# One projection tile for the attention keys instead of two, and the RWKV bonus sums issued earlier

## The chip, the cores and the metric

The kernel runs on one core of one Trainium2 chip. The time is the device time of one execution in microseconds (us); what is compared is the median over several executions. Engines are named as in the profile: PE is TensorE's matmul stream and PEld its weight loads, DVE is VectorE, ACT is ScalarE, POOL is GpSimd, and SP is the engine that here only issues DMAs.

## What is computed

The reference is one layer of a hybrid decoder on 512 tokens of width 1024. Cut to what matters here:

```
mod  = silu(c) @ ada_w + ada_b            # shift, scale and gate of both sub-layers
h    = x * (1 + scale1) + shift1
proj = h @ w_in                           # q 512 | k 128 | v 128 | rwkv r, k, v 3*512 | three loras 256
y_attn = sliding_window_attention(q, k, v)      # 8 heads of 64, grouped on 2 key/value heads
y_rwkv = rwkv7(...)                       # 8 heads of 64, ends in:
    bonus = sum(r * k * r_k, over the 64 of a head) * v
    y     = (group_norm(state output) + bonus) * g
x = LayerNorm(alpha * x + gate1 * (concat(y_attn, y_rwkv) @ w_out))
...                                       # then a PEER layer: top-16 of 128*128 experts, 8 heads
```

The keys have 128 columns, 64 for each of the two key/value heads. Heads of attention come in pairs on the two halves of the 128 partitions, so the score matmuls need each key head on both halves.

## The kernel before, in words

The program has three stages, each begun by an all-engine barrier: `emit_projections` (barrier L270, from 3 us), `emit_mixing` (barrier L881, from 192 us: attention and the RWKV recurrence) and `emit_experts` (barrier L1716, the rest). The change touches the first alone.

**Projection tiles.** `w_in` is worked off in TILES = 21 tiles of 128 columns, in this order: 14 RWKV tiles (j = 0 to 13), the values (j = 14, V_TILE), four query tiles (15 to 18, Q_TILE) and two key tiles (19 and 20, K_TILE). A key tile holds the 64 columns of one key head twice, loaded by two DMAs, so that its product has this head on both halves of the partitions. A tile is computed in split precision: SP loads `wt` (L294, or L290 for keys), ACT rounds it to `wth` (L429), DVE forms the remainder `wtl` (L721), and PE adds three times eight matmuls of 128x128x512: `wth` with `hi` (L563), `wth` with `lo` (L573), `wtl` with `hi` (L568). ACT copies the result out of its PSUM bank (L443 RWKV, L446 values, L448 queries, L450 keys); for RWKV tiles DVE then mixes it with the token before (L727). The three result banks are 0, 1 and 7.

**What is woven in.** The order on each engine is written out by hand, as `if j == ...` branches in the loop over tiles. An engine goes through its instructions in order, and semaphores tie the engines together. Near the change stand:

- *Key norms.* POOL squares `KN` (L385), PE sums the squares per head into bank 4 (`squares`, L595, at j = 13 and 14), DVE puts a floor under them (L761), ACT takes the root (L494, at j = 15), DVE the reciprocal (L818, at j = 16), and PE spreads the result to the rows of two pairs at j = 16 and of two at j = 17 (`norm_rows`, L606, banks 3 and 5). DVE's `normalised(p)` has three operations per pair of heads (L774, L777, L781).
- *Bonus.* POOL multiplies r and k (L391) into `tmp[2 + p % 2]`, two buffers for four pairs of heads p; DVE scales by `r_k` (`bonus_in`, L765); PE sums over each head (`bonus`, L615, banks 4 and 5), which are two matmul records per pair of heads; DVE multiplies by v (`bonus_out`, L770). PE issues `bonus` 0 and 1 at j = 18 and 2 and 3 behind the last tile.
- *Products with the decays.* Behind L391 POOL has four products for k (L396) and four for `AI` (L399), and DVE has four for r at j = 20 (L833).
- *Modulation of the second sub-layer.* DVE adds `ada_b` to 16 columns of bank 6 (L838, L839) behind its loop.

The two waits of POOL and PE around the bonus:

```
pool.wait_ge(bsum_up, START + p - 1)              # POOL, before the product of p = 2, 3 (L390)
pe.wait_ge(nk_up, START + 2 * (PAIRS - 1) + 1)    # PE, before bonus: banks 3 and 5 read (L612)
```

Of the kernel before, what the change touches and what calls it, by code (L numbers as in the profile page):

```python
# [8 lines left out]
P = 128  # L9
# [4 lines left out]
PAIRS = HEADS // 2  # L14
ATTN_COLS = 768
# [4 lines left out]
START = 8  # L20
# [172 lines left out]
def emit_projections(nc, banks, sem, v):  # L193
# [10 lines left out]
    with ctx:  # L204
# [23 lines left out]
        vT = asum[0]  # L228
        xin = [[qT[:, 2 * t + h, :] for h in range(2)] for t in range(2)] + [tmp[0:2], tmp[2:4]]
# [10 lines left out]
        gb_in, sink_in = sem("gb_in"), sem("sink_in")  # L240
# [25 lines left out]
        Q_TILE = V_TILE + 1  # L266
        K_TILE = Q_TILE + 4
        TILES = K_TILE + 2

# [4 lines left out]
        def _(sp):  # L274
# [9 lines left out]
            def weights(j):  # L284
                if j >= 2:
                    sp.wait_ge(wtl_up, START + j - 1)
                if j >= K_TILE:
                    n = j - K_TILE
                    for d in range(2):
                        sp.dma_start(wt[j % 2][:, :, 64 * d:64 * d + 64], wv[:, :, 512 + 64 * n:576 + 64 * n])\  # L290
                            .then_inc(wt_in[j % 2], 16)
                    return
                at = (ATTN_COLS + RWKV[j] * P if j < V_TILE else 640 if j == V_TILE else (j - Q_TILE) * P)
                sp.dma_start(wt[j % 2][:, :, :], wv[:, :, at:at + P]).then_inc(wt_in[j % 2], 16)  # L294
# [20 lines left out]
            for j in range(3, TILES):  # L315
                weights(j)
                if j in (5, 7, 9, 11):
                    ada_load((j + 7) // 2)
            sp.wait_ge(gb_in, START + 32)
# [3 lines left out]
        def _(pool):  # L323
# [63 lines left out]
            for p in range(PAIRS):  # L387
                pool.wait_ge(kp_up, START + PAIRS + p + 1)
                if p >= 2:
                    pool.wait_ge(bsum_up, START + p - 1)  # L390
                pool.tensor_tensor(tmp[2 + p % 2][:, :], PM[:, p, :], PM[:, 4 + p, :], ALU.mult).then_inc(rk_up, 1)  # L391
# [10 lines left out]
        def _(act):  # L402
# [22 lines left out]
            def rounded(j):  # L425
                act.wait_ge(wt_in[j % 2], START + 16 * (j // 2 + 1) + (16 if j >= K_TILE else 0))
# [11 lines left out]
            def evacuated(j):  # L438
                act.wait_ge(proj_up, START + j + 1)
                src = slots[j % 3][:, :]  # L440
                if j < V_TILE:
                    n = RWKV[j]
                    act.activation(PM[:, n, :], src, ACT.Copy, scale=omu[:, n:n + 1]).then_inc(proj_scaled, 1)  # L443
                elif j == V_TILE:
                    act.wait_ge(ada_used, START + len(pieces))
                    act.activation(vT[:, :], src, ACT.Copy).then_inc(proj_scaled, 1)  # L446
                elif j < K_TILE:
                    act.activation(qT[:, j - Q_TILE, :], src, ACT.Copy, scale=HD ** -0.5).then_inc(proj_scaled, 1)  # L448
                else:
                    act.activation(kT[:, j - K_TILE, P:], src, ACT.Copy).then_inc(proj_scaled, 1)  # L450

# [48 lines left out]
        def _(pe):  # L500
# [108 lines left out]
            def bonus(p):  # L609
                pe.wait_ge(rks_up, START + p + 1)  # L610
                pe.wait_ge(ss_max, START + 1)
                pe.wait_ge(nk_up, START + 2 * (PAIRS - 1) + 1)  # L612
                if p >= 2:
                    pe.wait_ge(bo_up, START + p - 1)
                pe.matmul(banks[4 + p % 2][:, :], diag2[:, :], tmp[2 + p % 2][:, :], start=True, stop=True)\  # L615
                    .then_inc(bsum_up, 1)
# [18 lines left out]
            for j in range(TILES):  # L635
# [10 lines left out]
                elif j == 16:  # L646
# [6 lines left out]
                    norm_rows(1)  # L653
                elif j == 17:
                    norm_rows(2)
                    norm_rows(3)
                elif j == 18:
                    bonus(0)
                    bonus(1)
            bonus(2)  # L660
            bonus(3)

        @block.vector
        def _(dve):
# [98 lines left out]
            def bonus_in(p):  # L763
                dve.wait_ge(rk_up, START + p + 1)
                dve.tensor_scalar(tmp[2 + p % 2][:, :], tmp[2 + p % 2][:, :], par[:, R_RK + p:R_RK + p + 1], None,  # L765
                                  ALU.mult).then_inc(rks_up, 1)

            def bonus_out(p):
                dve.wait_ge(bsum_up, START + p + 1)
                dve.tensor_tensor(BO[:, p, :], banks[4 + p % 2][:, :], PM[:, 8 + p, :], ALU.mult).then_inc(bo_up, 1)  # L770
# [22 lines left out]
            for j in range(TILES):  # L793
# [16 lines left out]
                elif j == 15:  # L810
                    floored()
                    bonus_in(0)
                    bonus_in(1)
                elif j == 16:
# [3 lines left out]
                    dve.reciprocal(norms, norms).then_inc(norms_up, 1)  # L818
                elif j == 17:
                    normalised(0)  # L820
                    normalised(1)
                elif j == 18:
                    normalised(2)
                    normalised(3)
                elif j == 19:
                    bonus_out(0)
                    bonus_in(2)
                    bonus_out(1)
                    bonus_in(3)
                elif j == 20:  # L830
# [1688 lines left out]
```

## Time and profile before

| | us |
|---|---|
| median of 3 runs (lowest, highest) | 1800.62 (1797.14, 1803.17) |
| the profiled execution | 1799.91 |
| its span, first to last instruction | 1798.2 |
| first projection tile starts on PE | 43.5 |
| barrier between projections and mixing is released | 192.1 |
| mean granted TensorE clock of the core | 0.987 |

The profiled execution's time is 1.7 us above its span, and 0.7 us below the median. A timeline row gives the start in us, the time until the end of the merged instructions, the engine, the line, the operation, the tiles it writes and reads, their count, and in brackets how long the engine sat idle before it and what ended that. PE's matmuls are pipelined, so that a row's time reaches a little into the next one's: starts are the surer measure.

### The profile page before, as it was taken

Reading aid. Unit: us, or ns where it says so; the run is one execution under the profiler, and the core shown is the slowest. Engines: PE = TensorE matmul, PEld = TensorE weight load, DVE = VectorE, ACT = ScalarE, POOL = GpSimd, SP = SyncE. Lnnn points to the kernel's source line nnn. Section 1 sums busy time; section 2 is a strip of 40 time slices with the busy share of each in tenths; the row PEclk is TensorE's granted clock in tenths of the full one; section 3 lists DMA queues with packets and bytes.
Section 4 is the critical chain, followed back from the end, with each engine's and each line's share of the span. In section 5 each row is a group of like instructions: output and inputs, shape, how many; then the busy total and the mean of one; then the engine's idle time right before and its main releaser. Section 6 shows DMA issues by size and latency. Waiting matters only on the chain.

```text
span 1798.2 us, 36538 instructions
## 1 busy us (share of the span) xinstructions
PE 1731.4 (96%) x12400; PEld 1515.6 (84%) x12400; DVE 1412.4 (79%) x2928; ACT 695.4 (39%) x1304; POOL 603.5 (34%) x481
## 2 busy tenths in 40 slices
PE   5999899889999999899999999999999999999996
PEld 3776788747999999899999999999888888888885
DVE  1885666646878888899999999687698888888877
ACT  3433455514444454433333333334343333333331
POOL 5012633303344353444333343353243332233200
PEclk8999999999999999999999999999999999999998
DMA  9841000254443434699999998999999999999981
GB/s 318 278 155 48 2 3 3 79 202 163 129 135 122 129 123 127 238 321 322 322 327 348 321 317 307 326 411 368 367 412 349 358 351 350 357 357 349 349 281 63
DMA packets 247871, 444.37 MB, mean 247 GB/s; under 512 B 85522, under 2 KB 158580, under 8 KB 247780
## 3 DMA queue, kind: packets, MB, share of 16 engines
q1 hardware_dynamic: 207968, 300.07, 48.0%
q0 software_dynamic: 39168, 142.62, 21.2%
q8 instruction: 50, 0.82, 0.2%
q10 hardware_dynamic: 644, 0.52, 0.2%
q14 instruction: 41, 0.34, 0.1%
HBM read 388.16 MB, written 54.53 MB: 246 GB/s over the span
## 4 chain that ended last, share of the span: by engine, by line
PE 73%; DMA 2%; DVE 1%; SPq 1%; ACT 1%; issue 0%; ACTq 0%; POOL 0%; DVEq 0%
PE bank L1489 26%; PE bank L2030 10%; PE bank L2031 10%; PE bank L2032 10%; PE bank L1469 6%; PE bank L1952 5%; PE bank L2009 4%; PE bank L1427 2%; DMA vsel<-in_peer_v,picks 1%; PE bank L1964 1%; SPq L1460 1%; DMA xrows<-xpicks 0%; DMA uraw<-in_peer_u,xrows 0%; DMA urows<-in_peer_u 0%; DVE n_stats L1393 0%
## 5 line engine op out<-in xcount | busy, mean ns | idle before, releaser
L1489 PE MATMUL bank<-hh,uh 128*128 128x368 f32 x1024 | 350.4, 342 | 0.0
L1489 PE MATMUL bank<-hl,uh 128*128 128x368 f32 x1024 | 337.4, 329 | 0.0
L2030 PE MATMUL bank<-vh,wh 128*128 128x512 f32 x768 | 299.8, 390 | 3.1 <-DVE wl L2443 3.1
L2031 PE MATMUL bank<-vl,wh 128*128 128x512 f32 x768 | 299.6, 390 | 0.0
L2032 PE MATMUL bank<-vh,wl 128*128 128x512 f32 x768 | 299.6, 390 | 0.0
L1547 POOL DMA_INDIRECT vsel<-in_peer_v,picks x128 | 154.2, 1204 | 406.8 <-DVE gt L1573 392.5
L2183 ACT ACTIVATE vh<-vraw 128x1024 fp32r<-128x1024 f32 x128 | 135.9, 1062 | 285.7 <-PE bank L2032 269.6
L1547 POOL DMA_INDIRECT wide<-in_peer_u,picks x108 | 152.6, 1413 | 202.3 <-DVE wide L1554 188.1
L2440 DVE TENSOR_TENSOR vl<-vraw,vh 128x1024 fp32r<-128x1024 f32 x128 | 156.5, 1223 | 80.2 <-ACT vh L2183 80.2
L1489 PEld LDWEIGHTS bank<-hl,uh 128*128 128x128 f32 x1024 | 193.1, 189 | 0.0
L1489 PEld LDWEIGHTS bank<-hh,uh 128*128 128x128 f32 x1024 | 192.8, 188 | 0.0
L1489 PE MATMUL bank<-hh,ul 128*128 128x368 f32 x1024 | 192.5, 330 | 0.0
L1489 PEld LDWEIGHTS bank<-hh,ul 128*128 128x128 f32 x1024 | 174.6, 189 | 0.0
L1573 DVE SCALAR_TENSOR_TENSOR gt<-vsel,wsel,gt 128x1024 f32<-128x1024 f32 x128 | 164.1, 1282 | 13.0 <-DMA vsel<-in_peer_v,picks 5.5
L2030 PEld LDWEIGHTS bank<-vh,wh 128*128 128x128 f32 x768 | 144.5, 188 | 33.5 <-DVE vl L2440 3.5
L2032 PEld LDWEIGHTS bank<-vh,wl 128*128 128x128 f32 x768 | 144.6, 188 | 30.0
L2031 PEld LDWEIGHTS bank<-vl,wh 128*128 128x128 f32 x768 | 144.7, 188 | 29.9
L1512 POOL TENSOR_TENSOR ul<-uraw,uh 128x1024 fp32r<-128x1024 f32 x41 | 99.1, 2416 | 189.6 <-ACT uraw L1504 189.6
L2162 ACT ACTIVATE SS<-bank 128x512 f32<-128x512 f32 x96 | 57.5, 599 | 254.8 <-PE bank L2009 254.8
L1497 ACT ACTIVATE uh<-bank 128x512 fp32r<-128x512 f32 x256 | 144.9, 607 | 25.3 <-PE bank L1469 14.2
L1520 DVE TENSOR_TENSOR ul<-bank,uh 128x512 fp32r<-128x512 f32 x174 | 111.7, 683 | 45.4 <-ACT uh L1497 45.0
L1469 PE MATMUL bank<-ident,urows 128*128 128x128 f32 x1024 | 133.2, 273 | 3.8 <-DVE ul L1520 1.6
(379 smaller groups left out, 2989.1 us busy)
## 6 DMA issues: line engine op xcount, KB each, us to landing
urows<-in_peer_u SPq DMA_DIRECT2D x128, 512.0 KB, 8.2
vraw<-in_peer_v SPq DMA_DIRECT2D x128, 512.0 KB, 6.3
scored<-act_out SPq DMA_DIRECT2D x128, 192.0 KB, 5.2
gates<-SS SPq DMA_DIRECT2D x16, 1536.0 KB, 14.7
gtile<-gates SPq DMA_DIRECT2D x32, 768.0 KB, 7.5
act_in<-scored SPq DMA_DIRECT2D x128, 192.0 KB, 6.3
wt<-in_w_in SPq DMA_DIRECT2D x19, 512.0 KB, 4.4
wq<-in_peer_wq SPq DMA_DIRECT2D x18, 512.0 KB, 3.9
```

Source lines behind the costliest of these rows:

```text
L1469: last = pe.transpose(self.banks[2 + h][:, k * P:(k + 1) * P], self.u[s][:, (4 * h + k) * P:(4 * h + k + 1) * P], self.ident[:, :])
L1489: last = pe.matmul(bank, u[:, k, :], h[:, k, 0:TU], start=(n == 0), stop=(n == 3 * KD - 1))
L1497: act.activation(self.uh[s % 2][:, 4 * h:4 * h + 4, :], self.banks[2 + h][:, :].rearrange("p (k e) -> p k e", k=4), ACT.Copy)\
L1512: pool.tensor_tensor(self.ul[s % 2][:, :, :], self.uraw[:, :, :], self.uh[s % 2][:, :, :].bitcast(F32), ALU.subtract).then_inc(self.ul_up, 1)
L1520: dve.tensor_tensor(self.ul[s % 2][:, 4 * h:4 * h + 4, :], self.banks[2 + h][:, :].rearrange("p (k e) -> p k e", k=4), self.uh[s % 2][:, 4 ...
L1547: pool.indirect_dma_start(out=into[:, :], out_offset=None, in_=row, in_offset=bass.IndirectOffsetOnAxis(ap=self.picks[:, at:at + 1], axis=0))\
L1573: dve.scalar_tensor_tensor(out=self.y[:, :], in0=self.vsel[k][:, :], scalar=self.wsel[:, k:k + 1], in1=self.y[:, :], op0=ALU.mult, op1=ALU ...
L2030: pe.matmul(b, wh[s][:, cols], vh[s][:, half], start=first, stop=False)
L2031: pe.matmul(b, wh[s][:, cols], vl[s][:, half], start=False, stop=False)
L2032: last = pe.matmul(b, wl[s][:, cols], vh[s][:, half], start=False, stop=stop)
L2183: act.activation(vh[s][:, :], vraw[s][:, :], ACT.Copy).then_inc(vh_up, 1)
L2440: dve.tensor_tensor(vl[s][:, :], vraw[s][:, :], vh[s][:, :].bitcast(F32), ALU.subtract)\
```

## The change

- The keys become one tile of 128 columns, at j = 15, ahead of the four query tiles; there are 20 tiles. ACT writes the product's lower half to head 0's place and its upper half to head 1's place in `kT`, in two instructions of 64 partitions. When both are written, SP copies each to the other half of the partitions by a DMA of 64 partitions x 512 values, and waits for both DMAs before the barrier.
- The products of r and k go to four buffers `rk` (tmp 2, 3, 0, 1). POOL's product for p = 2 and 3 no longer waits for a bonus sum, but for the sums of squares that read tmp 0 and 1.
- The bonus sums go to banks 4 and 6. PE issues 0 and 1 at j = 16, behind `norm_rows` 0 and 1, and 2 and 3 at j = 18. DVE's parts move along: the modulation of bank 6 to j = 15, `bonus_in` 2 and 3 to j = 16, `bonus_out` to j = 17 and 18, and the products of r with the decays from j = 20 to j = 19.

```diff
+        rk = tmp[2:4] + tmp[0:2]
-        Q_TILE = V_TILE + 1
-        K_TILE = Q_TILE + 4
-        TILES = K_TILE + 2
+        K_TILE = V_TILE + 1
+        Q_TILE = K_TILE + 1
+        TILES = Q_TILE + 4
...
 SP: weights(j)
-                if j >= K_TILE:
-                    n = j - K_TILE
-                    for d in range(2):
-                        sp.dma_start(wt[j % 2][:, :, 64 * d:64 * d + 64], wv[:, :, 512 + 64 * n:576 + 64 * n])\
-                            .then_inc(wt_in[j % 2], 16)
-                    return
...
+            sp.wait_ge(proj_scaled, START + K_TILE + 1)
+            for n in range(2):
+                here, other = (slice(64 * d, 64 * d + 64) for d in (n, 1 - n))
+                sp.dma_start(kT[other, n, P:], kT[here, n, P:]).then_inc(k_in, 16)
+            sp.wait_ge(k_in, START + 32)
             sp.wait_ge(gb_in, START + 32)
...
 POOL
                 if p >= 2:
-                    pool.wait_ge(bsum_up, START + p - 1)
-                pool.tensor_tensor(tmp[2 + p % 2][:, :], PM[:, p, :], PM[:, 4 + p, :], ALU.mult).then_inc(rk_up, 1)
+                    pool.wait_ge(ss_up, START + p + 1)
+                pool.tensor_tensor(rk[p][:, :], PM[:, p, :], PM[:, 4 + p, :], ALU.mult).then_inc(rk_up, 1)
...
 ACT: evacuated(j)
+                elif j == K_TILE:
+                    act.activation(kT[0:64, 0, P:], slots[j % 3][0:64, :], ACT.Copy)
+                    act.activation(kT[64:P, 1, P:], slots[j % 3][64:P, :], ACT.Copy).then_inc(proj_scaled, 1)
...
 PE: bonus(p), and the loop
-                pe.wait_ge(nk_up, START + 2 * (PAIRS - 1) + 1)
+                pe.wait_ge(cols_used, START + 3)
-                pe.matmul(banks[4 + p % 2][:, :], diag2[:, :], tmp[2 + p % 2][:, :], start=True, stop=True)\
+                pe.matmul(banks[4 + 2 * (p % 2)][:, :], diag2[:, :], rk[p][:, :], start=True, stop=True)\
...
                     norm_rows(1)
+                    bonus(0)
+                    bonus(1)
                 elif j == 17:
                     norm_rows(2)
                     norm_rows(3)
                 elif j == 18:
-                    bonus(0)
-                    bonus(1)
-            bonus(2)
-            bonus(3)
+                    bonus(2)
+                    bonus(3)
...
 DVE: the loop
                     bonus_in(1)
+                    dve.wait_ge(ada_used, START + 8)
+                    dve.tensor_tensor(mod[:, 16:32], banks[6][:, 16:32], par[:, R_ADAB + 24:R_ADAB + 40], ALU.add)\
+                        .then_inc(cols_used, 1)
+                    dve.wait_ge(cols_used, START + 3)
+                    dve.tensor_scalar(mod[:, 24:32], mod[:, 24:32], 1.0, None, ALU.add)
                 elif j == 16:
...
+                    bonus_in(2)
+                    bonus_in(3)
                 elif j == 17:
                     normalised(0)
                     normalised(1)
+                    bonus_out(0)
+                    bonus_out(1)
                 elif j == 18:
                     normalised(2)
                     normalised(3)
+                    bonus_out(2)
+                    bonus_out(3)
                 elif j == 19:
-                    bonus_out(0)
-                    bonus_in(2)
-                    bonus_out(1)
-                    bonus_in(3)
-                elif j == 20:
                     dve.wait_ge(rk_up, START + PAIRS)
                     for p in range(PAIRS):
                         dve.tensor_tensor(PM[:, p, :], PM[:, p, :], PD[:, p, :], ALU.mult)
...
-            step(dve.tensor_tensor(mod[:, 16:32], banks[6][:, 16:32], par[:, R_ADAB + 24:R_ADAB + 40], ALU.add))
-            dve.tensor_scalar(mod[:, 24:32], mod[:, 24:32], 1.0, None, ALU.add)
-            bonus_out(2)
-            bonus_out(3)
```

## Rows read from the trace of the kernel before

**Rows 1.** Busy time by stretch: us, engines busy (x instructions), PEclk, DMA, GB/s
```profile
45.00:188.00 143.00, 141.84 (x587) 105.72 (x586) 111.41 (x138) 51.00 (x66) 26.17 (x20) 0.98 0.48 151
188.00:192.00 4.00, 1.68 (x4) 0.38 (x2) 1.94 (x3) 0.59 (x1) 2.98 (x3) 1.00 0.00 0
192.00:340.00 148.00, 138.55 (x3455) 120.44 (x3456) 93.23 (x177) 82.96 (x213) 60.36 (x73) 1.00 0.01 3
```

**Rows 2.** Timeline, PE in the last two tiles
```profile
178.72 1.98 PE L573 MATMUL bank<-lo,wth 128*128 128x512 f32 x8
...
184.16 1.98 PE L573 MATMUL bank<-lo,wth 128*128 128x512 f32 x8
...
185.97 1.98 PE L568 MATMUL bank<-hi,wtl 128*128 128x512 f32 x8
```

**Rows 3.** Timeline, end of the stage, all engines
```profile
185.11 5.87 POOL L399 TENSOR_TENSOR AI<-AI,wide 128x512 f32<-128x512 f32 x4
...
187.79 1.88 PE L615 MATMUL bank<-tmp,diag 128*128 128x512 f32 x4
187.99 0.60 ACT L450 ACTIVATE kT<-bank 128x512 f32<-128x512 f32 x1 [4.85 <-PE bank L568]
...
189.71 0.69 DVE L770 TENSOR_TENSOR BO<-bank,PK 128x512 f32<-128x512 f32 x1 [0.17 <-PE bank L615]
...
192.16 1.05 POOL L932 TENSOR_TENSOR BHs<-AI,PL 128x512 f32<-128x512 f32 x1 [1.17 <-POOLq L881]
```

**Rows 4.** Waits of POOL, 28 to 197 us: in total, times, longest
```profile
POOL tmp L391 <- PE bank L615: 33.3, 1, 33.3
```

**Rows 5.** Timeline around tile 16, ACT, DVE and PE
```profile
151.51 0.60 ACT L448 ACTIVATE qT<-bank 128x512 f32<-128x512 f32 x1 [5.96 <-PE bank L568]
152.00 1.05 ACT L429 ACTIVATE wth<-wt 128x1024 fp32r<-128x1024 f32 x1
...
154.37 0.63 ACT L494 ACTIVATE rn<-rn 8x512 f32<-8x512 f32 x1
...
155.03 3.34 DVE L818 RECIPROCAL rn<-rn 8x512 f32<-8x512 f32 x1 [0.61 <-ACT rn L494]
...
156.76 0.60 PE L650 MATMUL bank<-ident,asum 128*128 128x128 f32 x4
...
158.51 1.95 PE L606 MATMUL bank<-rn,g 8*128 8x512 f32 x4 [1.16 <-DVE rn L818]
...
160.40 3.47 PE L563 MATMUL bank<-hi,wth 128*128 128x512 f32 x8
...
165.77 1.99 PE L568 MATMUL bank<-hi,wtl 128*128 128x512 f32 x8
```

**Rows 6.** Busy time by stretch, columns as in rows 1
```profile
162.00:164.00 2.00, 2.00 (x6) 1.62 (x5) 1.78 (x3) 0.00 (x0) 0.00 (x0) 0.50 0.00 0
```

**Rows 7.** Timeline, the first pair of bonus sums
```profile
171.55 1.98 PE L573 MATMUL bank<-lo,wth 128*128 128x512 f32 x8
...
175.18 1.88 PE L615 MATMUL bank<-tmp,diag 128*128 128x512 f32 x4
...
176.24 0.69 DVE L770 TENSOR_TENSOR BO<-bank,PK 128x512 f32<-128x512 f32 x1 [1.55 <-PE bank L615]
```

**Rows 8.** Timeline, second pair of sums of squares on PE
```profile
143.90 1.88 PE L595 MATMUL bank<-tmp,head_of 128*8 128x512 f32 x4
```

**Rows 9.** Products on DVE and POOL by line: ns min/median/max, first to last start
```profile
L833 DVE TENSOR_TENSOR PK<-PK,PD x4: 1770/1776/1778, 180.5 to 185.6; 128x512 f32<-128x512 f32 x4
...
L781 DVE TENSOR_TENSOR PK<-PK,wide x4: 691/691/695, 161.1 to 174.0; 128x512 f32<-128x512 f32 x4
...
L396 POOL TENSOR_TENSOR PK<-PK,wide x4: 1480/1610/1750, 178.8 to 183.4; 128x512 f32<-128x512 f32 x4
```

**Rows 10.** SP's last weight issues, and the landing of all 23 loads of `wt`
```profile
146.83 8.50 SPq L290 DMA_DIRECT2D wt<-in_w_in  x4
...
DMA to landing us min/median/max: 3.1/4.4/15.9
```

More of the change, by code:

```diff
@@ L239, in emit_projections @@
         wt_in = [sem(f"wt_in{i}") for i in range(2)]
-        gb_in, sink_in = sem("gb_in"), sem("sink_in")
+        gb_in, sink_in, k_in = sem("gb_in"), sem("sink_in"), sem("k_in")
         consts, rows_up, par_up, silu_up = sem("consts"), sem("rows_up"), sem("par_up"), sem("silu_up")
@@ L286, in weights @@
                     sp.wait_ge(wtl_up, START + j - 1)
-                if j >= K_TILE:
-                    n = j - K_TILE
-                    for d in range(2):
-                        sp.dma_start(wt[j % 2][:, :, 64 * d:64 * d + 64], wv[:, :, 512 + 64 * n:576 + 64 * n])\
-                            .then_inc(wt_in[j % 2], 16)
-                    return
-                at = (ATTN_COLS + RWKV[j] * P if j < V_TILE else 640 if j == V_TILE else (j - Q_TILE) * P)
+                at = (ATTN_COLS + RWKV[j] * P if j < V_TILE else {V_TILE: 640, K_TILE: 512}.get(j, (j - Q_TILE) * P))
                 sp.dma_start(wt[j % 2][:, :, :], wv[:, :, at:at + P]).then_inc(wt_in[j % 2], 16)
@@ L425, in rounded @@
             def rounded(j):
-                act.wait_ge(wt_in[j % 2], START + 16 * (j // 2 + 1) + (16 if j >= K_TILE else 0))
+                act.wait_ge(wt_in[j % 2], START + 16 * (j // 2 + 1))
                 if j >= 3:
@@ L446, in evacuated @@
                     act.activation(vT[:, :], src, ACT.Copy).then_inc(proj_scaled, 1)
-                elif j < K_TILE:
+                elif j == K_TILE:
+                    act.activation(kT[0:64, 0, P:], slots[j % 3][0:64, :], ACT.Copy)
+                    act.activation(kT[64:P, 1, P:], slots[j % 3][64:P, :], ACT.Copy).then_inc(proj_scaled, 1)
+                else:
                     act.activation(qT[:, j - Q_TILE, :], src, ACT.Copy, scale=HD ** -0.5).then_inc(proj_scaled, 1)
-                else:
-                    act.activation(kT[:, j - K_TILE, P:], src, ACT.Copy).then_inc(proj_scaled, 1)
             def gates_of(p):
@@ L764, in bonus_in @@
                 dve.wait_ge(rk_up, START + p + 1)
-                dve.tensor_scalar(tmp[2 + p % 2][:, :], tmp[2 + p % 2][:, :], par[:, R_RK + p:R_RK + p + 1], None,
+                dve.tensor_scalar(rk[p][:, :], rk[p][:, :], par[:, R_RK + p:R_RK + p + 1], None,
                                   ALU.mult).then_inc(rks_up, 1)
@@ L769, in bonus_out @@
                 dve.wait_ge(bsum_up, START + p + 1)
-                dve.tensor_tensor(BO[:, p, :], banks[4 + p % 2][:, :], PM[:, 8 + p, :], ALU.mult).then_inc(bo_up, 1)
+                dve.tensor_tensor(BO[:, p, :], banks[4 + 2 * (p % 2)][:, :], PM[:, 8 + p, :], ALU.mult).then_inc(bo_up, 1)
             def normalised(p):
```

## The prediction

> **What bounds the kernel now.** I first read the busy time by stretch. In the projections, 45 to 188 us, PE is busy 141.84 of 143 us, and no other engine is near that; then come 4 us in which PE does 1.68 us of work, and then mixing, which PE leads again [rows 1]. So a microsecond of PE work taken out of the projections moves the barrier by about as much, until another engine arrives at it last. Both later stages begin at barriers of their own and are unchanged: what is gained before 192 us is passed on whole, if nothing gives it back. The timeline of PE in the last tiles gives its pace: from one tile's second set of eight matmuls to the next one's is 184.16 - 178.72 = **5.44 us**, and a third of a tile is 185.97 - 184.16 = 1.81 us [rows 2].
>
> The end of the stage is not PE's, though. The last tile is done at 185.97 + 1.98 = 187.95; ACT's copy ends at 188.59, PE's last bonus sums at 189.67, DVE at 190.40, and POOL's four products at 185.11 + 5.87 = 190.98. POOL's next instruction starts 1.17 us after that, at 192.15 (the row says 192.16) [rows 3]. POOL is last by 3.03 us against PE's last tile. The waits of POOL tell why: 33.3 us for one bonus sum, before its third product of r and k [rows 4]. The eight products behind it run late, all beside DVE.
>
> The third place is around tile 16. PE ends its transposes at 157.36 and starts the normalisation rows at 158.51, having waited 1.16 us for DVE's reciprocal, which waited for ACT's root [rows 5]. The next tile then runs slower: from its first set to its third are 165.77 - 160.40 = 5.37 us where two thirds of a tile take 3.62 [rows 5, 2], and the granted clock there is 0.50, the 1.2 GHz level [rows 6]. This drop costs 1.75 us.
>
> **The change, part by part.** Against the profiled execution's 1799.91 us:
>
> 1. *One tile fewer.* PE loses 24 matmuls, **-5.44 us** [rows 2], and with it go a load, a rounding and a remainder that were hidden.
> 2. *POOL off the end.* Its third and fourth products now wait for the second pair of sums of squares, which PE starts at 143.90 [rows 8], so they run at about 145 to 148 and the products for k behind them at about 148 to 154 (four at 1.48 to 1.75 us [rows 9]). The products for `AI` follow DVE's normalisation and end with it, before tile 18 is done. What ends last is then ACT's copy of the last query tile, 0.64 us after PE (187.95 to 188.59 [rows 3]), and the barrier follows as before. The tail shrinks from 3.03 to 0.64 us: **-2.39 us**.
> 3. *Bonus sums inside the loop.* Both pairs of sums ran on PE before as well: one at j = 18, one behind the end. Now one is at j = 16 and one at j = 18, so PE's path gains one pair. Its price: from the second set of a tile to that of the next, with a pair between, are 178.72 - 171.55 = 7.17 us, less 5.44: **+1.74 us** with the rounding of the timestamps [rows 7, 2]. If the half clock doubled it, it would be 3.5; if it fills a wait, 0. It stands behind the wait, so I take 1.74.
> 4. *ACT's second instruction for the keys.* It stands ahead of the root on which the reciprocal and PE wait. ACT goes from one copy to the next in 152.00 - 151.51 = 0.49 us [rows 5]. A copy of 64 partitions is not in the trace; at worst it is a full one, 0.49, and at best nothing. I take the full one, since the length along the row is the same 512: the root, the reciprocal and PE's normalisation rows all come **+0.49 us** later, and PE idles 1.65 us.
> 5. *The copies of the keys.* SP has sent its last tile about 147 (its first issue in [rows 10] is tile 19's) and waits for ACT's second copy, near 152.6. Nothing is queued behind this wait but the barrier. No row shows a copy from SBUF to SBUF. The loads of `wt`, four times as large, land in 3.1 to 15.9 us [rows 10]; even two of 15.9 one after the other, which is unlikely, would end at 184.4, about when the stage now ends. Cost 0. The Trainium skill (DMA: Bandwidth & Descriptors, Anatomy of one DMA) fits about 2.0 us plus the bytes at 436 GB/s for a DMA of the other, GpSimd path, which would be some 2.3 us for such a copy of 128 KB.
> 6. *DVE's moved parts.* `bonus_in` 2 and 3 and two small operations on the modulation fall where DVE is idle or ahead; only two `bonus_in` stand between the reciprocal and the normalisation, and PE has another 5.44 us of tile 17 before it asks for what these make. What would be late next is DVE at the very end. Let S be PE's start of the second pair of bonus sums. DVE's first `bonus_out` starts at S + 1.06 (176.24 - 175.18), the second ends by S + 2.6, and four products at 0.69 us end by **S + 5.4** [rows 7, 9]. PE: next second set at S + 3.54 (178.72 - 175.18), third at S + 5.35, end at S + 7.33, ACT at **S + 7.97** [rows 7, 2, 3]. DVE is covered by 2.6 us.
>
> Sum: -5.44 - 2.39 + 1.74 + 0.49 = **-5.6 us**, that is 1794.3 us for the profiled execution. The median of the runs shown is 0.7 above it, so 1795.0.
>
> **The rivals.**
>
> *POOL's work collides with DVE's at the new place.* DVE's product of two SBUF tiles takes 691 ns alone and 1776 ns beside POOL's [rows 9]. If POOL were still at work when DVE does the four r products, they would end at S + 2.6 + 7.1 = S + 9.7, which is 1.7 us past ACT: -3.9, 1796.7 us. For it: POOL's `AI` products now run beside DVE's normalisation and stretch it. Against: there are 4 us of slack before tile 18 ends, and the operations with a PSUM operand do not stretch (0.69 us at 189.71 while POOL worked [rows 3]). Chance 0.12. The Trainium skill (GPSIMD Engine Reference, Specifications) says that GpSimd shares its SBUF interfaces with VectorE and contends with instructions of two SBUF inputs; by that rule this is where moving POOL's products could cost, and rows 9 agree with it in kind.
>
> *The clock drops once more, or for longer.* The pause before the normalisation rows grows from 1.16 to 1.65 us, and the one that there is already brought 1.2 GHz. One more such stretch costs 1.75 us: -3.85, 1796.8. Chance 0.15. The other way round, if the drop does not come (it follows a short pause, and the moment may matter), the gain is 7.35 us, 1793.3. Chance 0.08.
>
> *The gain is given back behind the barrier*, or the removed tile was covering something that the trace does not name: 0, 1800.6. Nothing in the profile speaks for it, since mixing needs nothing that arrives by time of day (DMA share 0.01 [rows 1]). Chance 0.07.
>
> *Slower.* The pause at the barrier makes PE enter mixing at 1.2 GHz. It now enters after 188 to 192, with 1.68 us of work in 4, at a clock of 1.00, and keeps 1.00 over 148 us [rows 1]. Now no bonus sums fill the pause. A microsecond at 1.2 GHz costs up to 0.5; the point from which it is a loss is 11.2 us at that level, and to be slower by over 0.3% it needs 22 of mixing's 148 us, with 1806 us if it takes 22. PE is busy 94% of mixing, which speaks against it. Chance 0.03.
>
> **How the numbers follow.** About 0.3%, 5.4 us, is what a measurement of this kernel can tell from no change, and my sum is -5.6. The forecast thus stands on the edge: 0.55 for it, with a range of its own of 1792 to 1798, since three runs of the same kernel lie 6 us apart. Half or a little more of this case, most of the case without a drop and a third of the two small-loss cases measure as faster: 0.47. The rest of these, and the case that gives nothing, is within 0.3%: 0.49. Slower: 0.04. The range takes in the two cases at 1796.7 and 1796.8 with the spread of the runs, and the one at 1793.3: 1791.0 to 1799.3.
>
> **What the changed profile should show.** PE's last L568 ends near 184.7; POOL is done before about 178; the last thing before the barrier is ACT's copy of qT; mixing starts near 186.6. L615 stands behind L606 at j = 16, and the normalisation rows start near 159.0. L833 takes 0.69 us each, and L781 or L777 partly more than now. The copies of kT land before 165. I am wrong if DVE or SP is last at the barrier, if a second stretch at 0.50 shows, if POOL still waits more than 10 us at the products of r and k, or if mixing becomes longer than it is.

## The result, and the profile after

The changed kernel takes **1789.66 us** (median of 6 runs, 1788.31 to 1793.62) against 1800.26 for the kernel before in the same rounds (6 runs, 1797.14 to 1803.17): ratio 0.9947, 95% interval 0.9936 to 0.9959. Over all comparisons of this study, 103 executions of the kernel before have a mean of 1799.3 us (standard deviation 2.0), and 21 of the changed kernel, among them eight of a copy that differs by two idle SP instructions, a mean of 1790.8 (2.3). So the change is worth **8.5 us**; the forecast was 5.6 us, 1795.0, with a low end of 1791.0. It is faster, by more than forecast. The two medians of six runs are 10.6 us apart; 2 us of that are chance, since the one lies 0.9 above the mean of all runs of its kernel and the other 1.1 below.

The profiled execution took 1790.5 us, with a span of 1788.8 and a mean granted clock of 0.986. Busy time by stretch, columns as in [rows 1]:

```profile
45.00:182.00 137.00, 134.89 (x563) 99.20 (x562) 107.84 (x136) 49.12 (x62) 30.57 (x22) 1.00 0.49 156
182.00:184.10 2.10, 0.32 (x6) 0.07 (x5) 0.00 (x0) 0.60 (x1) 0.05 (x1) 1.00 0.00 0
```

Projections are still PE's. The next fence is the timeline of the end of the stage, which answers to [rows 2, 3, 7].

```profile
174.95 1.88 PE L616 MATMUL bank<-tmp,diag 128*128 128x512 f32 x4
...
176.01 0.69 DVE L771 TENSOR_TENSOR BO<-bank,PK 128x512 f32<-128x512 f32 x1 [2.82 <-PE bank L616]
...
177.48 2.49 DVE L840 TENSOR_TENSOR PK<-PK,PD 128x512 f32<-128x512 f32 x4
...
180.31 1.98 PE L569 MATMUL bank<-hi,wtl 128*128 128x512 f32 x8
182.32 0.60 ACT L451 ACTIVATE qT<-bank 128x512 f32<-128x512 f32 x1 [6.57 <-PE bank L569]
...
184.05 1.05 POOL L935 TENSOR_TENSOR BHs<-AI,PL 128x512 f32<-128x512 f32 x1 [9.71 <-POOLq L884]
184.06 1.10 PE L1072 MATMUL bank<-PK,AI 64*64 64x128 f32 x32 [1.78 <-PEq L884]
```

POOL now waits 9.71 us for the barrier, DVE is done at 179.97, and ACT's last copy of `qT` comes last. From the end of PE's last tile (182.29) to the first matmul of mixing are 1.77 us; before they were 192.17 - 187.95 = 4.22 (187.95 by [rows 3], and this row of the kernel before). The products of r and the decays take 0.69 us each, where they took 1.78 [rows 9].

```profile
192.17 1.09 PE L1069 MATMUL bank<-PK,AI 64*64 64x128 f32 x30 [2.50 <-PEq L881]
```

The timeline around tile 16 answers to [rows 5].

```profile
150.45 0.59 ACT L448 ACTIVATE kT<-bank 64x512 f32<-64x512 f32 x1 [5.96 <-PE bank L569]
151.06 0.59 ACT L449 ACTIVATE kT<-bank 64x512 f32<-64x512 f32 x1
151.68 1.14 SPq L317 DMA_DIRECT2D kT<-kT  x2
...
154.71 3.34 DVE L824 RECIPROCAL rn<-rn 8x512 f32<-8x512 f32 x1 [0.61 <-ACT rn L495]
155.70 0.60 PE L651 MATMUL bank<-ident,asum 128*128 128x128 f32 x4
158.20 1.95 PE L607 MATMUL bank<-rn,g 8*128 8x512 f32 x4 [1.90 <-DVE rn L824]
160.08 1.98 PE L616 MATMUL bank<-tmp,diag 128*128 128x512 f32 x4
161.50 2.40 PE L564 MATMUL bank<-hi,wth 128*128 128x512 f32 x8
163.74 1.98 PE L574 MATMUL bank<-lo,wth 128*128 128x512 f32 x8
165.55 1.97 PE L569 MATMUL bank<-hi,wtl 128*128 128x512 f32 x8
```

PE's pause before the normalisation rows is 1.90 us (1.16 before), and the pair of bonus sums behind them moves the next set's start by 161.50 - 160.08 = 1.42 us. Tile 16 then runs at full pace: the first set to the third are 4.05 us where they were 5.37. The granted clock says why. These are two stretches of the changed kernel's first trace, and then the same stretches of a second trace of it (columns as in [rows 1]):

```profile
162.00:164.00 2.00, 2.00 (x11) 1.62 (x10) 1.93 (x3) 0.00 (x0) 1.37 (x2) 1.00 0.00 0
186.00:188.00 2.00, 2.00 (x20) 1.67 (x22) 1.97 (x4) 1.49 (x3) 1.94 (x5) 0.50 0.00 0
```

```profile
162.00:164.00 2.00, 2.00 (x4) 1.00 (x3) 1.93 (x4) 0.00 (x0) 1.37 (x2) 0.50 0.00 0
186.00:188.00 2.00, 2.00 (x41) 1.62 (x37) 0.95 (x2) 0.44 (x1) 2.00 (x3) 1.00 0.00 0
```

The same program was at 0.50 (1.2 GHz) behind the pause in one execution and behind the barrier in the other. One trace of it must not be read as the change's effect on the clock.

The copies of the keys, by line (the last line is from issue to landing):

```profile
L317 SPq DMA_DIRECT2D kT<-kT x2: 503/550/597, 151.7 to 152.2; - x2
...
DMA to landing us min/median/max: 2.2/2.3/2.3
```

They land by about 154.5, 30 us before the barrier, and the first matmul that reads `kT` starts at 194.0. The fit in the Trainium skill (DMA: Bandwidth & Descriptors, Anatomy of one DMA), which is for the other, GpSimd path, gives an estimate of 2.3 us for this size. On this path the trace agrees, with 2.2 to 2.3 us.

**The stages.** Since one trace differs from another, I took the same four cuts from every trace: PE's first projection tile, the end of the last tile's third set, the first matmul of mixing, and the experts' barrier. Means of five traces of the order of before (three of the kernel itself, and `before_filled` and `before_shifted` below, which do not move its work) and four of the changed kernel (one of them `after_shifted`):

| us | before | changed | difference | forecast |
|---|---|---|---|---|
| tiles | 144.9 | 141.4 | -3.6 | -3.2 |
| last tile's end to mixing | 4.2 | 1.8 | -2.4 | -2.4 |
| mixing | 189.0 | 187.3 | **-1.7** | 0 |
| experts | 1417.0 | 1416.9 | -0.1 | 0 |

The rest, -0.3, lies before the first tile. It is not told from chance: the first tile starts at 41.7 to 43.5 us in the five traces and at 41.9 to 42.6 in the four. Where both kernels ran tile 16 at 1.2 GHz, and without `before_filled`, which had two such stretches there, the tiles differ by 144.6 - 141.9 = 2.8 us (2.76 before rounding). The two terms that were forecast are there. A third, in a stage that neither edit touches, is not in the forecast.

### The profile page after: what moved, and what is told of

It reads as the page before. It is cut to its first block, busy times and chain, and to the rows that moved or that the text cites. A ratio compares the mean times of both kernels' runs of the same rounds, so it can differ in the third digit from the quotient of the medians.

```text
span 1788.8 us, 36485 instructions
## 1 busy us (share of the span) xinstructions
PE 1726.4 (97%) x12376; PEld 1511.8 (85%) x12376; DVE 1407.2 (79%) x2927; ACT 694.8 (39%) x1303; POOL 605.1 (34%) x481
## 4 chain that ended last, share of the span: by engine, by line
PE 75%; DVE 1%; DMA 1%; SPq 1%; ACT 0%; issue 0%; ACTq 0%; DVEq 0%
PE bank L1492 27%; PE bank L2033 10%; PE bank L2035 10%; PE bank L2034 10%; PE bank L1472 6%; PE bank L1955 5%; PE bank L2012 4%; PE bank L1430 2%; PE bank L1967 1%; SPq L1463 1%; DMA uraw<-in_peer_u,xrows 0%; DMA urows<-in_peer_u 0%; DMA xrows<-xpicks 0%; DVE n_stats L1396 0%; PE bank L1906 0%
## 5 line engine op out<-in xcount | busy, mean ns | idle before, releaser
L2035 PEld LDWEIGHTS bank<-vh,wl 128*128 128x128 f32 x768 | 144.9, 189 | 30.2
L2034 PEld LDWEIGHTS bank<-vl,wh 128*128 128x128 f32 x768 | 144.9, 189 | 30.2
```

The source lines that it names most:

```text
L2034: pe.matmul(b, wh[s][:, cols], vl[s][:, half], start=False, stop=False)
L2035: last = pe.matmul(b, wl[s][:, cols], vh[s][:, half], start=False, stop=stop)
```

## The experiments

**The same two programs again**, as a measure of the scatter.

`before_again`:

> The kernel before, unchanged, for a second trace and times. Two theories for the 4 to 5 us that my sum of -5.6 us misses. Theory R (systematic): a stretch of PE at 1.2 GHz behind the pause at tile 16 belongs to the kernel before and is gone after; then this trace shows granted clock 0.50 somewhere in 158 to 168 us again, and the last L568 comes about 1.8 us later against the first L553 than it would at full clock. Theory C (chance): where a short pause brings 1.2 GHz and where not changes from one execution to the next, as does the start of the first tile (43.48 us before, 42.40 us after); then the clock dips stand at other places here. Time: ratio 1.000 within 0.2%.

Measured: 1798.88 us (11 runs), ratio 1.0000 (0.9990 to 1.0009).

`after_again`:

> The changed kernel, unchanged, for a second trace and times. Theory R: no stretch at 0.50 in 156 to 168 us, as in its first trace; theory C: such a stretch shows in some execution, and this trace's parts (start to first tile, first tile to barrier, mixing) differ from the first trace's 42.4, 141.7 and 187.5 us by 1 us and more. Time ratio to before: 0.9947 again (1789 to 1792 us) under both, 0.9969 if the first measurement was lucky.

Measured: 1790.73 us (6 runs), ratio 0.9949 (0.9932 to 0.9967). The effect is firm. The stretch at 1.2 GHz at tile 16 is back (the second pair of rows above), and the tiles took 142.1 us instead of 139.9.

**Each part alone.** `tile_only` is the kernel before with the one key tile, its two ACT copies and the DMAs, and the bonus work in its old order:

```diff
-        Q_TILE = V_TILE + 1
-        K_TILE = Q_TILE + 4
-        TILES = K_TILE + 2
+        K_TILE = V_TILE + 1
+        Q_TILE = K_TILE + 1
+        TILES = Q_TILE + 4
...
+            for n in range(2):
+                here, other = (slice(64 * d, 64 * d + 64) for d in (n, 1 - n))
+                sp.dma_start(kT[other, n, P:], kT[here, n, P:]).then_inc(k_in, 16)
```

> The key tile and its DMA copies as in the change, the bonus sums, buffers and waits as before. My terms: PE is 5.4 us shorter, but POOL's third product of r and k still waits for the first bonus sum at j = 18, and behind it stand 14.6 us of POOL's work, of which two tiles covered 11.6 before and now one tile covers 6.2. So the stage ends with POOL at about 191 to 192 us as before, and the kernel gains nothing: ratio 0.999 to 1.001 (1798 to 1802 us). The rival, that a tile of PE is worth its time by itself: ratio 0.997 (1795 us).

Measured: 1798.05 us (11 runs), ratio 0.9993 (0.9983 to 1.0003). Taking a tile of 5.44 us out of the engine that bounds the stage gives 1.3 us by the means, which is **nothing that this measurement can tell from zero**. The timeline of its end shows why:

```profile
180.19 6.79 DVE L832 TENSOR_TENSOR PK<-PK,PD 128x512 f32<-128x512 f32 x4
180.67 1.53 PE L568 MATMUL bank<-hi,wtl 128*128 128x512 f32 x6
...
184.73 5.82 POOL L398 TENSOR_TENSOR AI<-AI,wide 128x512 f32<-128x512 f32 x4
...
191.76 1.56 PE L1068 MATMUL bank<-PK,AI 64*64 64x128 f32 x24 [7.84 <-PEq L880]
```

PE is done at 182.2, and the stage ends when POOL does, at 190.55, as it did before (190.98 [rows 3]). The wait of 33.3 us for the first bonus sum [rows 4] sets POOL's end, whatever PE does behind that sum.

`bonus_only` is the other part alone, with 21 tiles: four buffers, POOL's wait on `ss_up`, banks 4 and 6, and PE's and DVE's new places:

```diff
-                    pool.wait_ge(bsum_up, START + p - 1)
+                    pool.wait_ge(ss_up, START + p + 1)
...
+                    bonus(0)
+                    bonus(1)
```

> The buffers, waits, banks and places of the bonus sums as in the change, the keys in two tiles at the end as before. My terms: tail -2.4 us, a pair of bonus sums more in the loop +1.7 us: -0.7 us, ratio 0.9996 (1799.5 us). If the change also takes a stretch at 1.2 GHz away by issuing bonus sums behind the normalisation rows (theory R placed in this part): -2.4 us, ratio 0.9986 (1797.8 us), and no 0.50 in 156 to 168 us. If the extra gain of the change sits in this part altogether: -5 us, ratio 0.997.

Measured: 1797.29 us (11 runs), ratio 0.9987 (0.9978 to 0.9996). The forecast for it was -0.7 us. The cut from the last tile to mixing is 1.76 us, as in the full change, and the tiles are 146.7 us, 1.8 above the mean of before, which is the pair of sums; mixing took 187.4 us, 1.6 below before, and that is about the part that the forecast lacks. The two parts give -1.3 and -2.4 us by their means, and together -8.5. They are not a sum: the tile is worth nothing while POOL ends the stage, and with POOL off the end it takes the tiles from 146.7 to 141.4 us.

**POOL late again, with everything else of the change.** `late_pool`:

```diff
             pool.wait_ge(exp_up, START + 3)
+            pool.wait_ge(bsum_up, START + 4)
             for p in range(PAIRS):
```

> The changed kernel with one wait added: POOL's eight products with the decays wait for the last bonus sum (at j = 18), so that POOL ends the stage again. POOL then starts at about 177 and needs 10 to 12 us: the barrier comes at about 189, 5 us later than in the changed kernel, of which PE is idle. Theory of the tail alone: 5 us slower than the changed kernel (1795 us, ratio 0.9975). If PE's idle time at the barrier also brings 1.2 GHz into mixing (as 0.50 from 187.7 to 198.0 us in the kernel with the tile alone): up to 2 us more, 1797 us, and a stretch at 0.50 shows behind the barrier.

Measured: 1799.92 us (12 runs), ratio 1.0005 (0.9996 to 1.0013). One line takes the whole gain away. The cut from the last tile to mixing is 7.6 us instead of 1.8, and the line for DVE's products shows the collision with POOL that was my first rival (the second line is POOL's products for k, beside it):

```profile
L841 DVE TENSOR_TENSOR PK<-PK,PD x4: 1334/1759/1779, 179.3 to 183.9; 128x512 f32<-128x512 f32 x4
L397 POOL TENSOR_TENSOR PK<-PK,wide x4: 1295/1724/1751, 178.7 to 183.4; 128x512 f32<-128x512 f32 x4
```

The longer cut explains 5.8 of the 9.1 us by which it exceeds the changed kernel. Mixing is 1.4 us longer too, 1.04 of it at its very start, at 0.50. So I asked whether the clock behind a longer pause makes the rest.

**PE kept busy through the pause.** `late_filled` adds to `late_pool` 24 matmuls that write a bank nobody reads:

```diff
+            pe.wait_ge(nk_up, START + 2 * PAIRS)
+            for i in range(24):
+                pe.matmul(banks[3][:, :], wth[0][:, i % KD, :], hi[:, i % KD, :], start=True, stop=True)
```

> The kernel of late_pool (1799.9 us, 9.4 us above the changed kernel though its barrier comes only 5.8 us later by the traces) with 24 more matmuls of PE behind the last tile, which add 5.4 us of work that nobody reads, while PE waits for POOL. Clock theory: the 3 to 4 us that the pause costs beyond its length are 1.2 GHz behind the barrier; with PE busy up to it there is no 0.50 between 185 and 200 us, and the kernel is 1 to 3 us faster than late_pool, 1797 to 1799 us, in spite of more work. Rival, the extra is chance or sits elsewhere: 1799.9 us as late_pool, or slower by what the matmuls outlast POOL.

Measured: 1799.38 us (11 runs), ratio 1.0003 (0.9993 to 1.0013). The stretch at 0.50 behind the barrier is gone, and the first part of mixing is back from 37.28 to 36.23 us. Mixing took 186.6 us instead of 188.7; the other half of this difference lies at its end, where the stretch at 0.50 was shorter (3.4 us instead of 6.8). The mean fell by 0.35 us only, and a gain of 1 us at the start is inside the scatter of these runs: they neither show nor exclude that the clock there costs the whole kernel as much as it costs the stage.

`before_filled` adds six such matmuls to the end of the kernel before's projections, under its barrier pause.

> The kernel before with 6 more matmuls (1.4 us) behind the last bonus sum, in the 2.5 us in which PE waits at the barrier. Clock theory: PE's pause there brings 1.2 GHz into mixing in some executions (one of three traces, 1.0 us each); filled, the mean falls by 0.3 to 1 us, ratio 0.9995 to 0.9998. Rival: no effect, ratio 1.000. A mean lower by 2 us or more would say that most of the change's extra gain is the clock behind the barrier.

Measured: 1799.23 us (11 runs), ratio 1.0005 (0.9994 to 1.0016). No effect that can be measured, and mixing took 188.9 us, as in the kernel before. So PE's idle time at the barrier was not what made most of mixing's difference; for a stretch at 0.50 at its start, which two of the other four traces of this order have, one trace cannot tell.

**A third trace of each.** `before_third`:

> The kernel before, once more, for a third trace. If the parts that differ between its traces (first tile at 43.48 and 42.95 us, barrier to first mixing chunk's end 39.2 and 40.3 us) are chance, they come out anywhere in 41.5 to 44 and 39.2 to 40.5 here; if the changed kernel's earlier first tile (42.4, 41.9) is systematic, this one is again at 43 or later.

Measured: 1798.31 us. `after_third`:

> The changed kernel once more, for a third trace. First tile: at 41.5 to 42.5 us if the earlier start belongs to kernels of 20 tiles (six of six at 42.40 or before, four of four kernels of 21 tiles at 42.23 or later). A stretch at 0.50 behind the pause of tile 16 shows in it with about even chance; without it the parts from first tile to barrier take 141.7 us, with it 143.9 us.

Measured: 1790.14 us. At tile 16 the clock was at 0.50 again in both, and the first tile started at 42.23 and 42.44 us, so an earlier start does not belong to the changed kernel. Mixing took 188.7 and 186.5 us.

**The pause at tile 16.** `root_early` is the changed kernel with ACT's root moved ahead by one tile, and DVE's reciprocal with it (and the copy of `PL`, which had stood ahead of it):

```diff
-                elif j == 15:
+                elif j == 14:
                     act.wait_ge(ss_max, START + 1)
...
+                    dve.wait_ge(exp_up, START + 3)
+                    dve.tensor_copy(PL[:, :, :], PD[:, :, CH - 1::CH])
                     bonus_in(0)
...
-                elif j == 16:
-                    dve.wait_ge(exp_up, START + 3)
-                    dve.tensor_copy(PL[:, :, :], PD[:, :, CH - 1::CH])
                     dve.wait_ge(ss_root, START + 1)
                     dve.reciprocal(norms, norms).then_inc(norms_up, 1)
+                elif j == 16:
```

> The changed kernel with ACT's root at j = 14 instead of j = 15 (ahead of its two key copies) and DVE's reciprocal at j = 15, so that the reciprocal is ready about 154 us, before PE asks for it at 156.3. Theory P: PE's pause of 1.9 us before the normalisation rows is a term of the path; it goes, and the first normalisation row follows the transposes within 0.7 us: 1.9 us faster than the changed kernel. Theory P plus clock: the stretch at 1.2 GHz behind it (seen in every trace but the first of the changed kernel) goes as well, 1.75 us more: ratio to before 0.993 to 0.994 (1786.5 to 1788.5 us). Rival: DVE's reciprocal of 3.3 us delays its own remainders, so that PE waits there instead, and the ratio stays 0.995.

Measured: 1788.19 us (6 runs), ratio 0.9938 (0.9924 to 0.9951). Its timeline:

```profile
151.24 3.33 DVE L823 RECIPROCAL rn<-rn 8x512 f32<-8x512 f32 x1
...
155.37 0.60 PE L651 MATMUL bank<-ident,asum 128*128 128x128 f32 x4
...
155.89 1.98 PE L607 MATMUL bank<-rn,g 8*128 8x512 f32 x4
...
157.80 1.98 PE L616 MATMUL bank<-tmp,diag 128*128 128x512 f32 x4
...
159.22 2.41 PE L564 MATMUL bank<-hi,wth 128*128 128x512 f32 x8
```

PE does not pause, and there is no stretch at 0.50 at tile 16. The tiles take 138.3 us, 3.0 below the changed kernel's mean (141.36 - 138.31). The time is 2.4 us below by the means; the two intervals overlap, so the sign rests on the trace.

`bonus_first` lets the bonus sums run in the pause:

```diff
-                    norm_rows(0)
-                    norm_rows(1)
                     bonus(0)
                     bonus(1)
+                    norm_rows(0)
+                    norm_rows(1)
```

> The changed kernel with bonus sums 0 and 1 ahead of the normalisation rows at j = 16, so that 1.7 us of PE's pause of 1.9 us is filled with work that is needed anyway. Path theory: 1.7 us faster than the changed kernel, ratio to before 0.994 (1789 us); with the clock no longer dropping behind the pause up to 3.5 us, ratio 0.993. Rival: the clock drops just the same, since before the rows PE does only small work, and the gain is 1.7 us or less.

Measured: 1788.65 us (6 runs), ratio 0.9945 (0.9932 to 0.9959). The sums fill the pause, of which the profile leaves 0.19 us, and yet the stretch at 0.50 stayed (at 160.6 to 164.0):

```profile
156.03 1.88 PE L616 MATMUL bank<-tmp,diag 128*128 128x512 f32 x4
158.10 1.95 PE L607 MATMUL bank<-rn,g 8*128 8x512 f32 x4 [0.19 <-DVE rn L824]
```

So the pause is not the whole condition for the stretch; what else `root_early` changed that matters stays open. The time cannot be told from the changed kernel's.

`root_filled` is `root_early` with three matmuls of the kind above behind PE's last tile:

> The kernel of root_early (1788.2 us) with 3 more matmuls (0.7 us) behind the last tile, beside ACT's last copy. They end with ACT's copy, so the barrier moves by 0 to 0.3 us. Clock theory: PE's pause at the barrier of about 1.8 us is cut to 1.1, and 1.2 GHz behind the barrier, seen in one of five traces with the short tail, gets rarer: 1787.5 to 1788.5 us. Otherwise as root_early or 0.3 us slower.

Measured: **1785.32 us** (5 runs), ratio 0.9929 (0.9915 to 0.9942), the lowest of all. That the three matmuls add to `root_early` is not shown, since the intervals overlap. The version to keep is `root_early`.

**Where mixing lost its 1.7 us.** The stage can be cut by lines that every kernel has: its first matmul, the first product into `S`, the last of them, the last product of the group norm (L1304 before, L1307 in the changed kernel), and DVE's leaving the experts' barrier.

| us, one trace each | start to first S | to last S | to last norm | to barrier |
|---|---|---|---|---|
| before, first trace | 36.22 | 125.81 | 12.31 | 14.58 |
| before_again | 37.27 | 125.89 | 12.31 | 13.93 |
| before_third | 36.23 | 125.90 | 12.32 | 14.21 |
| before_filled | 36.23 | 125.84 | 12.31 | 14.56 |
| before_shifted (below) | 37.28 | 125.85 | 12.31 | 13.62 |
| changed, first trace | 36.24 | 125.85 | 12.32 | 12.97 |
| after_again | 36.24 | 125.96 | 12.32 | 13.23 |
| after_third | 36.22 | 125.83 | 12.32 | 12.14 |
| after_shifted (below) | 36.24 | 125.95 | 12.32 | 13.25 |
| tile_only | 37.47 | 125.83 | 12.32 | 13.08 |
| bonus_only | 36.23 | 125.82 | 12.31 | 13.05 |

Two things vary, and the 160 us between them do not. The first column takes 1 us more where the stage begins at 0.50. Two of the five traces of the order of before have that, none of the changed kernel's four, which makes 0.4 us of the difference. The last column makes the rest: its mean is 14.2 us in the order of before and 12.9 in the changed one, and in one trace of each either part of the change is enough to shorten it. In that column PE waits for the load of `w_out`: in all sixteen traces its first row of the product starts 0.09 us after the last of the eight transfers has landed. In the traces of the kernel before and of the changed kernel, SP's eight issues of this load, their landing, and PE's first rows of the product:

```profile
L919 SPq DMA_DIRECT2D PK<-in_w_out x8: 341/441/1522, 348.5 to 353.3; - x8
DMA to landing us min/median/max: 3.8/7.1/10.8
...
364.15 16.37 PE L1427 MATMUL bank<-PK,wide 128*128 128x512 f32 x32 [5.35 <-issue]
```

```profile
L922 SPq DMA_DIRECT2D PK<-in_w_out x8: 349/442/862, 340.4 to 343.7; - x8
DMA to landing us min/median/max: 3.6/7.4/10.4
...
354.26 16.64 PE L1430 MATMUL bank<-PK,wide 128*128 128x512 f32 x32 [3.51 <-issue]
```

The last of the eight goes out 4.8 us after the first before, and 3.3 us after it in the changed kernel: in the former the second issue takes 1.52 us in place of 0.44, and the third is late by that. From the first issue to the last landing are 15.6 us in this trace, and 13.7 in the changed kernel's. PE's idle time is longer by 1.84. SP waits for nothing there that the profile shows, so I supposed that it belongs to the place of the instruction in SP's stream, and shifted the stream alone. `before_shifted` (six increments) and `after_shifted` (two, which gives the changed kernel as many SP instructions ahead of this load as the kernel before):

```diff
             sp.wait_ge(sink_in, START + 16)
+            for _ in range(6):
+                sp.sem_inc(spare, 1)
```

> The kernel before, with six increments of a semaphore that nobody waits for, on SP ahead of the barrier. They do no work on the path and shift SP's later instructions by six. In the three traces of the kernel before, SP's third of eight issues of the w_out load came about 1.1 us late (0.39, then 1.2 to 1.6, then 0.48 us from one to the next); in the changed kernel the gaps were even. Theory A, the late issue belongs to the place of the instruction in SP's stream: here the eight issues take about 4.2 us, not 4.8, or the late one falls at another of the eight, the first output row starts 13.6 to 14.4 us after the first issue, the mixing stage takes about 187.3 us where the kernel before takes 188.9, and the mean time is 1.0 to 1.6 us below the kernel before. Theory B, the 1.5 us of the mixing stage are not from SP's stream but from what the removed tile left behind (the place of the 1.2 GHz stretches, memory traffic): the late third issue stays or the mixing stage keeps 188.5 to 189.4 us, time as the kernel before. Theory C, scatter only: the stage falls anywhere between 187 and 189.

Measured: 1799.74 us (11 runs), ratio 1.0003 (0.9991 to 1.0015).

> The changed kernel, with two increments of a semaphore that nobody waits for, on SP ahead of the barrier: SP then has as many instructions ahead of the w_out load as the kernel before. Theory A, place in the stream: the third of the eight issues is late again by about 1.1 us, the mixing stage goes from 187.2 to about 188.7 us, and the mean time is 1791.5 to 1792 where the changed kernel has 1790.3. Theory B, not from SP's stream: gaps stay even and the mixing stage at 186.5 to 187.8 us, mean 1790.3. Theory C, scatter: either.

Measured: 1791.38 us (8 runs), ratio 0.9959 (0.9947 to 0.9970). The rows of both, in this order:

```profile
L922 SPq DMA_DIRECT2D PK<-in_w_out x8: 340/433/1242, 349.0 to 353.1; - x8
DMA to landing us min/median/max: 4.0/6.6/10.3
...
363.49 16.67 PE L1430 MATMUL bank<-PK,wide 128*128 128x512 f32 x32 [4.13 <-issue]
```

```profile
L925 SPq DMA_DIRECT2D PK<-in_w_out x8: 348/449/877, 342.7 to 346.1; - x8
DMA to landing us min/median/max: 3.6/7.5/10.4
...
356.67 16.82 PE L1433 MATMUL bank<-PK,wide 128*128 128x512 f32 x32 [3.61 <-issue]
```

In `before_shifted` the fourth of the eight is late instead of the third, PE's idle time falls to 4.13 us, and the last column to 13.62, below the four others of its order. In `after_shifted` two instructions more did not bring a late third issue back (column 13.25), so the count of SP's instructions is not the cause by itself.

The length of the load goes with which of the eight is late. I took that from each of the sixteen traces, with the time from the first issue to the last landing:

| late issue | traces | first issue to last landing, us |
|---|---|---|
| the third, by 0.7 to 1.1 | before, before_again, before_third, before_filled | 14.8 to 15.6 |
| the fourth, by 0.5 to 1.0 | before_shifted, bonus_only, late_filled | 14.2 to 14.4 |
| the fifth or a later one, or none | the other nine, all four of the changed kernel among them | 13.5 to 14.0 |

The groups do not overlap. It is not the time between the first issue and the last: that is 4.1 us in `before_shifted` and in `after_again`, whose load took 14.4 and 13.6 us. The mean of the load is 15.0 us in the five traces of the order of before and 13.8 in the four of the changed one, so it makes 1.2 of mixing's 1.7 us, and the first column 0.4. That a late issue lengthens the load is read from which traces go together; no run delays one issue and nothing else.

The shift of `before_shifted` shortened the load by 0.8 us against the mean of the other four. The time of the whole kernel cannot tell whether this was passed on, since its interval reaches from 1.6 us faster to 2.7 slower; this trace also began mixing at 0.50, which cost 1 us. The experts' stage alone took 1413.8 to 1419.3 us over the sixteen traces, with no edit in it. What makes one issue late, and at which place, stays **open**.

## Why the prediction was wrong

The sign was right, and the size was not: 8.5 us against 5.6. The median of 1789.66 lies 5.3 us below the forecast and 1.3 below the low end. Not all of that is the mechanism: 1.3 us come from the level that the sum was taken from (1800.6, a median of three, where 103 runs have 1799.3), 1.1 from the six runs that made the median (1789.7, where 21 have 1790.8), and 2.9 from the gain itself. With another draw of runs it would have been on the edge of the range; the gain would still have been half as large again as the sum.

- *Step 1, one tile fewer, and step 3, the pair inside the loop*: right. Together with step 4 they come to -3.2 in the sum, and to -3.6 in the traces (-2.8 like with like; the 0.8 between them is where the half clock happened to fall). The pair cost 1.68 us where 1.74 was taken: from the normalisation rows to the tile's second set are 5.54 us with the pair (j = 16) and 3.86 without it (j = 17), in the changed kernel's first trace.
- *Step 2, POOL off the end*: right to a tenth, -2.4 us. POOL's third product of r and k waits 2.0 us, not 33.3, and what ended last was ACT's copy of `qT`. The argument that both edits need each other was in the sum without being said; `tile_only` and `late_pool` show it.
- *Step 4, ACT's second instruction*: right in kind, small in size. A copy of 64 partitions takes 0.59 us, as a full one, and what follows on ACT starts 0.61 to 0.62 later, not 0.49, both times. The pause grew by 0.74 us, from 1.16 to 1.90.
- *Step 5, the copies of the keys*: right, and far from the bound of 15.9 us each that I had reckoned with: 2.2 to 2.3.
- *Step 6, DVE covered*: right. It ends at S + 5.0 (179.97 - 174.95), the forecast was S + 5.4, and PE at S + 7.3.
- *The rivals*: the collision did not come, because POOL's last product ended at 174.3. That it would be real is shown by `late_pool`. The stretch at tile 16 neither doubled nor went away: it comes in three of the changed kernel's four traces. In the first it stood behind the barrier instead, from 185.6 us, and cost nothing there (36.24 us to the first S, as without it).

**The step that failed** is the sentence that both later stages "are unchanged: what is gained before 192 us is passed on whole". Mixing came out shorter in every pair of traces, by 0.9 to 2.9 us and by 1.7 in the mean: 1.2 us because PE waits there for the load of `w_out`, which took 13.8 us where it had taken 15.0, and 0.4 us because two of five traces of the order of before begin the stage at 1.2 GHz. The prediction looked at this stage for ways in which it might give time back (0.07 for that, 0.03 for the clock), with a DMA share of 0.01 as the reason that nothing there waits for a transfer; but that row ends at 340 us and the load runs from 348 to 364. It had no way in which the stage might give more. Why the load is shorter in the new program stays open. The rest of the 2.9 us is 0.4 in the tiles, 0.3 before the first tile, and about 0.4 between the sum of the stages (8.1) and the mean of the runs (8.5), none of it more than the scatter. The range failed with it: two cases that cost 1.8 us stood in it, and on the fast side only the one without the drop.

## What to carry to other kernels

Where two engines end a stage within a few microseconds of each other, work taken from the earlier one is worth nothing until the later one is moved too: the edits alone gave 1.3 us (not told from zero) and 2.4, both together 8.5, and a single wait put back gave it all away. Before a tile is taken out of the engine that is busy 99% of a stage, read who arrives at the barrier last, and what that engine had waited for. And when a stage is called unchanged, look for a wait in it that no work of the stage explains, such as PE's 5.35 us for a load. Its length here was not the same in programs that do the same work in the stage, and a range should be left open by that much on both sides.

## What the runs showed of the hardware that was not expected

- One program has stretches at 0.50 in different places from one execution to the next: behind the pause of 1.9 us at tile 16 in three traces, behind the barrier in the fourth. Where the normalisation rows follow the transposes at once (`root_early`, `root_filled`) there was none at tile 16; with a pause of 1.2 us (five traces of the order of before) always one, and also in `bonus_first`, where work filled the pause to 0.19 us.
- A copy on ACT of 64 partitions by 512 takes 0.59 us, and one of 128 partitions 0.60.
- A DMA from SBUF to SBUF of 64 partitions by 512 values lands 2.2 to 2.3 us after its issue.
- Of eight like DMA issues on SP, one can take 0.9 to 1.6 us in place of 0.44, with nothing that the profile shows to wait for. A late third issue went with a load of 14.8 to 15.6 us, a late fifth to eighth one with 13.5 to 14.0, as with none.
